# One kernel, three places: order of the prologue's sums, one padded row per channel block in the even convolution, and layer norm and rotation in one stage

## The chip, the core and the metric

The kernel runs on one core of one Trainium2 chip. The metric is the time of one launch in microseconds, as the device counts it. The core has five engines that work side by side and meet at semaphores: TensorE (PE: matmuls), VectorE (DVE), ScalarE (ACT), GpSimd (POOL) and SyncE (SP, which here only issues DMAs).

## What is computed

Two models of two layers each run one after the other on the same latent sequence (512 tokens of width 1024; the first model has 256 context tokens besides). The change touches only what comes ahead of the first layer's attention. In the reference that is:

```python
def layer_norm(x, g, b):
    xf = x.astype(F32)
    mu = jnp.mean(xf, axis=-1, keepdims=True)
    var = jnp.mean(jnp.square(xf - mu), axis=-1, keepdims=True)
    y = (xf - mu) * lax.rsqrt(var + EPS)
...
def conformer_conv(p_glu, conv_w, conv_b, ln_g, ln_b):
    a, gate = jnp.split(p_glu, 2, axis=-1)
    u = depthwise_conv(a * jax.nn.sigmoid(gate), conv_w, conv_b)
    return jax.nn.silu(layer_norm(u, ln_g, ln_b))
...
def even_mixer(h_lat, h_ctx, rope, w_in, ...):
    p_lat = h_lat @ w_in
    conv_lat = conformer_conv(p_lat[..., :EV_Q0], conv_w, conv_b, ln_g, ln_b)
    q_lat = apply_axial_rope(qk_heads(p_lat[..., EV_Q0:EV_K0]), rope)
    k_lat = apply_axial_rope(qk_heads(p_lat[..., EV_K0:EV_V0]), rope)
    v_lat = v_heads(p_lat[..., EV_V0:])
...
    conv_ctx = conformer_conv(p_ctx[..., :EV_Q0], conv_w, conv_b, ln_g, ln_b)
```

The depthwise convolution has 31 taps and 512 channels, and runs over the 512 latent tokens and over the 256 context tokens apart, each padded with zeros. The other part that matters is independent of the tokens: filters of the second layer's long convolution (`hyena_filters`: two small matmuls with sines, a third matmul, a decay and a division by the sum of magnitudes).

## The kernel before

Channels lie on the 128 partitions and tokens along the free dimension, so 512 channels are four blocks `c`. The program is a row of stages. A stage is a block of instruction streams, one for each engine; at its end all engines meet at a barrier, and inside it they meet only at semaphores. Each engine runs its own stream strictly in the order written, so an instruction that waits holds up all behind it on its engine. There is no planner: the order is the order of the code.

**Prologue** (`prologue`, line 1172, until 149.3 us of the trace). TensorE transposes the tokens, and between transposes it makes the filters: `filter(pe, u)`, line 1078, for u = 0 to 15, two matmul instructions into one of two banks. For each u VectorE multiplies by the decay (L1093), ScalarE takes magnitudes (L1106) and VectorE adds them up (L1116); GpSimd adds and subtracts pairs of filters (L1124). Filter u waits until VectorE has taken filter u - 2. Eight squares of the input follow, one for each block of 128 of the 1024 channels: ScalarE squares one into `squares` (L1259, two slots), and TensorE sums it over channels (`sum_blocks`, L518). In the loop over c the order is: square c, then magnitude 6 + c on ScalarE; sum c, then filter 6 + c on TensorE. `first.multiply` (L863) makes the first modulation products from weights in a ring of three tiles.

**Convolution stage** (`products`, called by `even_mixer`, until 368.2 us). TensorE multiplies the normed input by w_in in 20 units of weights, in float32 by three products of rounded halves. For each unit VectorE rounds the weights (`high`, L329), GpSimd makes the rest (`low`, L398), and TensorE waits for `low` (L458); VectorE converts two units ahead. Units 0 to 7 are value and gate of the four channel blocks, 8 to 15 q and k, 16 to 19 v. On odd units from 3 on TensorE also does a piece of modulation (L863, L876). The function `convolve` is called on VectorE once in each unit, and in units 2 to 18 it does 15 of the 248 steps of the convolution: for each block 31 taps, each in two instructions (L788: source times weight plus accumulator; L791 for the first), one for the latent row `pad_lat` (512 wide) and one for the context row `pad_ctx` (256 wide). The two rows take turns, so that a tap waits for the instruction two before it.

**Norm and rotation.** `layer_norm_silu` (L1516 to L1554) is one stage: sums over channels by TensorE, mean and centring by VectorE, squares by ScalarE, their sums, root and reciprocal, scaling and SiLU. Then a stage loads three tables (perm, cos, sin), and `swap_rotate` is another one: for each of eight items (four blocks of q, four of k, 512 wide) TensorE swaps partners with a matmul by `perm` (L1351) and VectorE does x = x cos + swapped sin in three instructions (L1360, L1361, L1362), of which each waits for the one before. The attention stage (L1403 on) follows at 423.8 us.

## Time and profile before

| | us |
|---|---|
| median of three runs | 4256.18 (4255.96 to 4268.26) |
| the profiled execution: time of the run | 4263.13 |
| the profiled execution: span | 4261.3 |
| TensorE busy / VectorE busy / ScalarE busy / GpSimd busy | 3766.9 / 2068.4 / 868.2 / 1400.6 |
| prologue | 0 to 149.3 |
| start of the products to the end of the convolution | 149.3 to 368.2 |
| norm, table loads, rotation | 368.2 to 423.7 |
| all that the change leaves as it is | 423.7 to 4261.3 |

The span begins with the first instruction and ends with the last; the run's own time is 1.8 us more. TensorE is busy for 88% of the span, so over the whole program it is the engine to look at, but the stretches that the change touches are a tenth of the span and have limits of their own. A share of busy time says nothing of them. The trace is read there stage by stage: what the engine that closes the stage waited for last.

### The profile page before, as it was taken

Reading aid. Unit: us, or ns where it says so; the run is one execution under the profiler, and the core shown is the slowest. Engines: PE = TensorE matmul, PEld = TensorE weight load, DVE = VectorE, ACT = ScalarE, POOL = GpSimd, SP = SyncE. Lnnn points to the kernel's source line nnn. Section 1 sums busy time; section 2 is a strip of 40 time slices with the busy share of each in tenths; the row PEclk is TensorE's granted clock in tenths of the full one; section 3 lists DMA queues with packets and bytes.
Section 4 is the critical chain, followed back from the end, with each engine's and each line's share of the span. In section 5 each row is a group of like instructions: output and inputs, shape, how many; then the busy total and the mean of one; then the engine's idle time right before and its main releaser. Section 6 shows DMA issues by size and latency. Waiting matters only on the chain. (4 is left out here: it accounts for less than half of the span.)

```text
span 4261.3 us, 46015 instructions
## 1 busy us (share of the span) xinstructions
PE 3766.9 (88%) x18394; PEld 2961.1 (69%) x18394; DVE 2068.4 (49%) x3150; ACT 868.2 (20%) x1681; POOL 1400.6 (33%) x606
## 2 busy tenths in 40 slices
PE   5896878999989889976999899968999888889998
PEld 2584357888878678845878566757888566667887
DVE  2697644224447456655233467845123377753122
ACT  2211412110011233311100244421000344501001
POOL 1221015225554200004455322225445322245444
PEclk9998969999999979988999899989999899989999
DMA  3440601221213100011333121113332221123332
GB/s 109 150 156 28 235 30 55 63 61 55 69 46 89 47 1 1 1 60 59 99 94 99 54 81 45 45 50 89 95 94 79 65 67 50 30 74 89 99 94 70
DMA packets 400355, 306.83 MB, mean 72 GB/s; under 512 B 11228, under 2 KB 367782, under 8 KB 399559
## 3 DMA queue, kind: packets, MB, share of 16 engines
q1 hardware_dynamic: 397896, 303.11, 23.6%
q8 instruction: 149, 2.44, 0.2%
q10 hardware_dynamic: 2239, 0.71, 0.1%
q14 instruction: 71, 0.58, 0.0%
HBM read 297.48 MB, written 6.29 MB: 71 GB/s over the span
## 5 line engine op out<-in xcount | busy, mean ns | idle before, releaser
L398 POOL TENSOR_TENSOR low<-raw,high 128x1024 fp32r<-128x1024 f32 (+1 forms) x437 | 1058.8, 2424 | 1398.6 <-DVE high L329 1398.6
L458 PE MATMUL scores<-high 128*128 128x512 f32 (+1 forms) x2496 | 962.0, 385 | 123.4 <-POOL low L398 106.8
L458 PE MATMUL scores<-low,high 128*128 128x512 f32 (+1 forms) x2496 | 947.7, 380 | 0.0
L458 PE MATMUL scores<-high,low 128*128 128x512 f32 (+1 forms) x2496 | 945.6, 379 | 0.0
L329 DVE CAST high<-raw 128x1024 fp32r<-128x1024 f32 (+1 forms) x437 | 415.7, 952 | 689.5 <-PE scores L458 374.5
L458 PE MATMUL bank<-high 128*128 128x512 f32 (+1 forms) x1760 | 648.5, 368 | 3.4 <-POOL low L398 3.4
L458 PE MATMUL bank<-low,high 128*128 128x512 f32 (+1 forms) x1760 | 648.1, 368 | 0.0
L458 PE MATMUL bank<-high,low 128*128 128x512 f32 (+1 forms) x1760 | 647.3, 368 | 0.0
L458 PEld LDWEIGHTS scores<-high 128*128 128x128 f32 x2496 | 481.3, 193 | 229.9 <-POOL low L398 116.0
L458 PEld LDWEIGHTS scores<-high,low 128*128 128x128 f32 x2496 | 479.9, 192 | 90.1
L458 PEld LDWEIGHTS scores<-low,high 128*128 128x128 f32 x2496 | 481.9, 193 | 85.5 <-issue 0.5
L458 PEld LDWEIGHTS bank<-high 128*128 128x128 f32 x1760 | 331.8, 189 | 63.3 <-POOL low L398 3.8
L458 PEld LDWEIGHTS bank<-high,low 128*128 128x128 f32 x1760 | 331.6, 188 | 56.1
L458 PEld LDWEIGHTS bank<-low,high 128*128 128x128 f32 x1760 | 332.0, 189 | 55.2
L677 ACT ACTIVATE raw<-x_all 128x512 f32<-128x512 f32 (+1 forms) x64 | 42.1, 681 | 1310.1 <-POOL low L398 1235.3
L351 POOL TENSOR_TENSOR low<-mix,high 128x1536 fp32r<-128x1536 f32 (+1 forms) x6 | 27.0, 4504 | 708.7 <-DVE high L340 708.7
L1592 DVE TENSOR_TENSOR hid<-hid 128x512 f32<-128x512 f32 x96 | 62.3, 649 | 329.9 <-ACT hid L1588 329.9
L351 POOL TENSOR_TENSOR low<-hid,high 128x1024 fp32r<-128x1024 f32 (+2 forms) x36 | 146.6, 4073 | 201.8 <-DVE high L340 201.8
L788 DVE SCALAR_TENSOR_TENSOR conv<-pad_lat,params,conv 128x512 f32<-128x512 f32 x120 | 99.4, 828 | 0.0
L788 DVE SCALAR_TENSOR_TENSOR conv<-pad_ctx,params,conv 128x256 f32<-128x256 f32 x120 | 76.0, 633 | 0.0
L1484 DVE TENSOR_REDUCE mx<-scores 128x1 f32<-128x768 f32 (+1 forms) x48 | 37.2, 775 | 74.6 <-PE scores L1403 74.5
L687 POOL TENSOR_TENSOR raw<-raw 128x512 f32<-128x512 f32 (+1 forms) x40 | 57.1, 1428 | 29.6 <-ACT raw L677 26.6
(575 smaller groups left out, 4350.3 us busy)
## 6 DMA issues: line engine op xcount, KB each, us to landing
raw<-in_mlp_w SPq DMA_DIRECT2D x128, 512.0 KB, 4.0
raw<-in_w_in SPq DMA_DIRECT2D x76, 512.0 KB, 3.9
ring<-in_ada_w SPq DMA_DIRECT2D x32, 1024.0 KB, 7.1
raw<-in_w_gate SPq DMA_DIRECT2D x44, 512.0 KB, 3.9
raw<-in_w_up SPq DMA_DIRECT2D x44, 512.0 KB, 3.9
raw<-in_w_down SPq DMA_DIRECT2D x40, 512.0 KB, 3.5
mix<-in_ada_w SPq DMA_DIRECT2D x16, 1024.0 KB, 7.3
raw<-in_od_w_in SPq DMA_DIRECT2D x29, 512.0 KB, 3.9
```

Source lines behind the costliest of these rows:

```text
L329: dve.tensor_copy(tile(high, u), tile(raw, u)).then_inc(high_ready, 1)
L351: return eng.tensor_tensor(low_, act, high, ALU.subtract)
L398: pool.tensor_tensor(tile(low, u), tile(raw, u), tile(high, u).bitcast(F32), ALU.subtract)\
L458: mm = pe.matmul(out(p), stationary, moving, start=(k0 + k == 0 and i == 0), stop=(k0 + k == job.kc - 1 and i == len(pairs) - 1))
L677: act.activation(self.tile(c), self.x[:, c, 0:self.width], ACT.Square).then_inc(self.squared, 1)
L687: pool.tensor_tensor(self.tile(0), self.tile(0), self.tile(c), ALU.add).then_inc(self.added, 1)
L788: ins = dve.scalar_tensor_tensor(out=out, in0=part, scalar=w[:, j:j + 1], in1=out, op0=ALU.mult, op1=ALU.add)
L1484: step(dve.tensor_reduce(mx[:, u % 2, mp:mp + 1], scores(mp), AX.X, ALU.max))
L1592: return dve.tensor_tensor(hid[:, c, t0:t0 + tn], hid[:, c, t0:t0 + tn], hid[:, c, t0:t0 + tn], ALU.mult)
```

## The change

**Prologue.** `squares` gets six slots where it had two. ScalarE takes magnitude u first and then squares block u - 6; TensorE makes filter u first and sums block u - 8. The first modulation product stands after filter 10 and not after filter 13.

**Convolution.** Latent and context rows of a channel block lie in one padded row, `pad`: 15 zeros, 512 tokens, 30 zeros, 256 tokens, 15 zeros. One instruction does a tap over 798 elements (the 30 between the rows are computed too and used by nobody). Even taps accumulate in `conv`, odd ones in `odd_taps`, and a last addition joins them: 32 steps for each block, 128 in all, 8 for each unit, in units 2 to 17. Odd taps read a copy of the row that ScalarE has shifted by one element (new class `ShiftedRows`: four copies of 826 elements, in units 1, 5, 9 and 13, two slots that lie in the room of v). For that reason the first write of v waits until the convolution has ended.

**Norm and rotation.** `norm_and_rotate` replaces both functions and the stage that loaded tables. SyncE loads the tables while the norm runs. GpSimd does x cos (eight operations), VectorE the other two of each item, and the items are put into gaps of the norm: three swaps ahead of the sums of squares, five behind. The norm works on rows of 798 with zeros in the gap of mean and reciprocal root.

The core of the diff:

```diff
@@ prologue
-        squares = tok[:, 0:2, 0:TA]
+        squares = tok[:, :, 0:TA]
...
-                for c in range(DC):
-                    if c >= 2:
-                        act.wait_ge(x_summed, c - 1)
-                    act.activation(squares[:, c % 2, :], x[:, c, :], ACT.Square).then_inc(x_squared, 1)
-                    hyena_filters.magnitudes(act, NT + c)
-                for u in range(NT + DC, FilterSpectra.N):
+                for u in range(NT, FilterSpectra.N):
                     hyena_filters.magnitudes(act, u)
+                    c = u - NT
+                    if c < DC:
+                        if c >= NT:
+                            act.wait_ge(x_summed, c - NT + 1)
+                        act.activation(squares[:, c % NT, :], x[:, c, :], ACT.Square).then_inc(x_squared, 1)
...
-                for c in range(DC):
-                    pe.wait_ge(x_squared, c + 1)
-                    sum_blocks(pe, m, squares[:, c % 2, :], (LAT, CTX), c == 0, c == DC - 1).then_inc(x_summed, 1)
-                    hyena_filters.filter(pe, NT + c)
-                first.multiply(pe, 0)
-                hyena_filters.filter(pe, NT + DC)
-                hyena_filters.filter(pe, NT + DC + 1)
+                for u in range(NT, FilterSpectra.N):
+                    hyena_filters.filter(pe, u)
+                    if u == NT + 4:
+                        first.multiply(pe, 0)
+                    c = u - NT - 2
+                    if c >= 0:
+                        pe.wait_ge(x_squared, c + 1)
+                        sum_blocks(pe, m, squares[:, c % NT, :], (LAT, CTX), c == 0, c == DC - 1).then_inc(x_summed, 1)
                 first.multiply(pe, 1)
@@ norm_and_rotate
+    segs = ((0, T), (T + GAP, TC))
...
+            issue(sp, [(perm[:, :], A["c_perm_e"]), (cos[:, :], A["c_cos_e"]), (sin[:, :], A["c_sin_e"])], tables_loaded)
...
+            for i, x in enumerate(items):
+                pool.wait_ge(swapped, i + 1)
+                pool.tensor_tensor(x, x, cos[:, :], ALU.mult).then_inc(weighed, 1)
...
+            def swap(i):
+                if i >= 2:
+                    pe.wait_ge(partners_weighed, i - 1)
+                pe.matmul(m.bank[4 + i % 2][:, :], perm[:, :], items[i], start=True, stop=True).then_inc(swapped, 1)
...
+            def weigh_partner(i):
+                dve.wait_ge(swapped, i + 1)
+                if i >= 2:
+                    dve.wait_ge(rotated, i - 1)
+                dve.tensor_tensor(part[:, i % 2, :], m.bank[4 + i % 2][:, :], sin[:, :], ALU.mult)\
+                    .then_inc(partners_weighed, 1)
+
+            def rotate(i):
+                dve.wait_ge(partners_weighed, i + 1)
+                dve.wait_ge(weighed, i + 1)
+                dve.tensor_tensor(items[i], items[i], part[:, i % 2, :], ALU.add).then_inc(rotated, 1)
...
@@ ShiftedRows.scalar
+        c = (u - 1) // 4
+        if u % 4 == 1 and c < 4:
+            if c == 0:
+                act.wait_ge(self.free, 32)
+            elif c >= 2:
+                act.wait_ge(self.convolved, self.steps * (c - 1))
+            self.stored(act, 2 * c + 1, 0, 1)
+            n = self.rows.shape[2]
+            act.activation(self.rows[:, c % 2, :], self.pad[:, c, 1:1 + n], ACT.Copy).then_inc(self.shifted, 1)
@@ even_mixer
+                        def values(act, c, b, y):
+                            if b == 0:
+                                act.wait_ge(copies.convolved, len(steps))
+                            return act.activation(v[:, b, :], y, ACT.Copy)
...
-                        steps = [(c, n) for c in range(4) for n in range(2 * CW)]
+                        steps = [(c, n) for c in range(4) for n in range(CW + 1)]
...
+                                base, acc = (CW + 1) * c, (conv[:, c, :], odd_taps[:, :])
+                                at = min(n, CW - 1)
+                                src = shifted[:, c % 2, at - 1:at - 1 + TG] if at % 2 else pad[:, c, at:at + TG]
...
+                                elif n < CW:
+                                    dve.wait_ge(convolved, base + n - 1)
+                                    ins = dve.scalar_tensor_tensor(out=acc[n % 2], in0=src, scalar=w, in1=acc[n % 2],
+                                                                   op0=ALU.mult, op1=ALU.add)
+                                else:
+                                    dve.wait_ge(convolved, base + n)
+                                    ins = dve.tensor_tensor(acc[0], acc[0], acc[1], ALU.add)
```

What stands in a row on TensorE in the prologue, from the last but one sum on, before (L1078 is a filter, L518 a sum, L863 a modulation product, L1131 the sum of magnitudes):

```order
L518 MATMUL scores<-tok,ones 32x128 x6
L1078 MATMUL scores<-hy_w_102,hy_hid 128x512
L863 MATMUL bank<-ring,cond 32x512 x8
L1078 MATMUL scores<-hy_w_102,hy_hid 128x512 x2
L863 MATMUL bank<-ring,cond 32x512 x8
L1131 MATMUL bank<-hy_total,ones 128x512
```

and after the change, from filters 5 to 8 on (L1080 is a filter, L520 a sum, L865 a modulation product):

```order
L1080 MATMUL scores<-hy_w_102,hy_hid 128x512 x4
L520 MATMUL scores<-tok,ones 32x128 x6
L1080 MATMUL scores<-hy_w_102,hy_hid 128x512
L520 MATMUL scores<-tok,ones 32x128 x6
L1080 MATMUL scores<-hy_w_102,hy_hid 128x512
L865 MATMUL bank<-ring,cond 32x512 x8
```

The sums now stand two filters behind, and the first modulation product has moved up. On VectorE one unit of the convolution stage has, before, a weight conversion (L329) and then pairs of the two rows:

```order
L329 CAST high<-raw 128x1024
L791 TENSOR_SCALAR conv<-pad_lat,params 128x512
L791 TENSOR_SCALAR conv<-pad_ctx,params 128x256
L788 SCALAR_TENSOR_TENSOR conv<-pad_lat,params,conv 128x512
L788 SCALAR_TENSOR_TENSOR conv<-pad_ctx,params,conv 128x256
```

and after it (L331 is the conversion):

```order
L331 CAST high<-raw 128x1024
L1780 TENSOR_SCALAR conv<-pad,params 128x798
L1785 TENSOR_SCALAR odd_taps<-qkv,params 128x798
L1788 SCALAR_TENSOR_TENSOR conv<-pad,params,conv 128x798
L1788 SCALAR_TENSOR_TENSOR odd_taps<-qkv,params,odd_taps 128x798
```

Where a unit had 15 such steps it has 8 wider ones. On VectorE in the norm, before:

```order
L1530 TENSOR_SCALAR mean<-scores 128x512
L1530 TENSOR_SCALAR mean<-scores 128x256
L1534 TENSOR_TENSOR conv<-conv,mean 128x768 x4
L1538 RECIPROCAL rstd<-rstd 128x512
L1538 RECIPROCAL rstd<-rstd 128x256
L1541 TENSOR_TENSOR conv<-conv,rstd 128x768 x4
```

and after it:

```order
L1554 TENSOR_TENSOR conv<-conv,mean 128x798 x4
L1539 TENSOR_TENSOR part<-bank,sin 128x512 x2
L1545 TENSOR_TENSOR qkv<-qkv,part 128x512
L1539 TENSOR_TENSOR part<-bank,sin 128x512
L1545 TENSOR_TENSOR qkv<-qkv,part 128x512
L1561 RECIPROCAL rstd<-rstd 128x512
L1561 RECIPROCAL rstd<-rstd 128x256
L1565 TENSOR_TENSOR conv<-conv,rstd 128x798 x4
L1539 TENSOR_TENSOR part<-bank,sin 128x512
```

Five of VectorE's sixteen rotation steps stand between centring and reciprocal, eleven behind the scaling; none of them is the product with cos, which is GpSimd's now.

## Rows read from the trace of the kernel before

**Rows 1.** Windows: stretch, busy us of each engine (instructions), TensorE clock, DMA share, GB/s

```profile
52.70:102.20 49.50, 31.90 (x133) 10.34 (x132) 14.08 (x23) 12.16 (x18) 11.48 (x8) 1.00 0.08 27
235.00:368.20 133.20, 125.32 (x719) 100.49 (x718) 133.16 (x211) 16.00 (x30) 32.76 (x12) 1.00 0.35 111
368.20:423.70 55.50, 27.36 (x48) 10.93 (x48) 29.95 (x36) 10.88 (x12) 0.00 (x0) 0.73 0.03 11
380.00:385.00 5.00, 3.95 (x5) 1.85 (x6) 0.12 (x1) 2.26 (x3) 0.00 (x0) 0.50 0.00 0
```

**Rows 2.** Timeline of PE, prologue: start us, us, what [idle before <-releaser]

```profile
55.05 1.07 PE L518 MATMUL scores<-tok,ones 128*32 128x128 f32 x12 [2.27 <-ACT tok L1259]
...
60.30 1.07 PE L518 MATMUL scores<-tok,ones 128*32 128x128 f32 x12 [2.18 <-ACT tok L1259]
...
94.78 3.64 PE L863 MATMUL bank<-ring,cond 128*32 128x512 f32 x16
...
98.35 3.78 PE L1078 MATMUL scores<-hy_w,hy_hid 64*128 64x512 f32 x4
```

**Rows 3.** Timeline of ACT, the same stretch

```profile
58.88 0.63 ACT L1106 ACTIVATE qkv<-hy_filt 128x512 f32<-128x512 f32 x1 [3.98 <-DVE hy_filt L1093]
59.42 0.83 ACT L1259 ACTIVATE tok<-x_all 128x768 f32<-128x768 f32 x1
```

**Rows 4.** Tile conv, 180 to 370 us: count, duration ns min/median/max, starts, forms

```profile
L788 DVE SCALAR_TENSOR_TENSOR conv<-pad_lat,params,conv x120: 732/740/2894, 190.5 to 366.9; 128x512 f32<-128x512 f32 x120
L788 DVE SCALAR_TENSOR_TENSOR conv<-pad_ctx,params,conv x120: 468/474/2622, 191.2 to 367.6; 128x256 f32<-128x256 f32 x120
...
L791 DVE TENSOR_SCALAR conv<-pad_lat,params x4: 532/536/543, 187.7 to 327.2; 128x512 f32<-128x512 f32 x4
```

**Rows 5.** Timeline of all engines around one and the last weight conversion

```profile
212.83 0.69 DVE L329 CAST high<-raw 128x1024 fp32r<-128x1024 f32 x1 [1.24 <-DMA raw<-in_ev_w_in]
...
213.61 2.83 POOL L398 TENSOR_TENSOR low<-raw,high 128x1024 fp32r<-128x1024 f32 x1 [12.91 <-DVE high L329]
...
214.10 2.62 DVE L788 SCALAR_TENSOR_TENSOR conv<-pad_ctx,params,conv 128x256 f32<-128x256 f32 x1
...
353.19 0.68 DVE L329 CAST high<-raw 128x1024 fp32r<-128x1024 f32 x1
```

**Rows 6.** Waits of PE, 183 to 368 us: us in total, times, longest

```profile
PE scores L458 <- POOL low L398: 5.5, 4, 1.8
```

**Rows 7.** Timeline of PE and DVE, norm stage

```profile
368.97 7.09 PE L1516 MATMUL scores<-conv,ones 128*128 128x512 f32 x16 [3.18 <-PEq L79]
...
381.05 8.26 PE L1522 MATMUL scores<-sq,ones 128*128 128x512 f32 x16 [4.99 <-ACT sq L1547]
...
376.56 3.56 DVE L1534 TENSOR_TENSOR conv<-conv,mean 128x768 f32<-128x768 f32 x4
...
388.35 5.14 DVE L1538 RECIPROCAL rstd<-rstd 128x512 f32<-128x512 f32 x2 [8.22 <-ACT rstd L1550]
...
393.52 3.57 DVE L1541 TENSOR_TENSOR conv<-conv,rstd 128x768 f32<-128x768 f32 x4
```

**Rows 8.** Timeline of PE and DVE, rotation, and PE's first row of attention

```profile
403.39 3.75 PE L1351 MATMUL scores<-qkv,perm 128*128 128x512 f32 x4 [14.07 <-PEq L79]
...
407.67 1.12 PE L1351 MATMUL scores<-qkv,perm 128*128 128x512 f32 x2 [0.53 <-DVE qkv L1362]
...
406.19 0.69 DVE L1361 TENSOR_TENSOR qkv<-qkv,cos 128x512 f32<-128x512 f32 x1
...
423.77 2.94 PE L1403 MATMUL scores<-qkv 64*128 64x512 f32 x8 [4.08 <-PEq L79]
```

**Rows 9.** Timeline of POOL in the prologue, and of DVE beside a POOL operation

```profile
53.59 2.87 POOL L1124 TENSOR_TENSOR mix<-hy_filt 128x512 f32<-128x512 f32 x2 [4.94 <-DVE hy_filt L1093]
...
163.76 1.39 DVE L605 SCALAR_TENSOR_TENSOR mix<-x_all,gain,bank 128x512 f32<-128x512 f32 x2
...
163.25 1.74 POOL L638 TENSOR_TENSOR low<-mix,high 128x512 fp32r<-128x512 f32 x1
```

More of the change, by code:

```diff
@@ L35 @@
 CW = 31
+GAP = 2 * (CW // 2)
+TG = T + GAP + TC
 HY_FFN = 64
@@ L1339, in _ @@
                                                   in1=small.norm_g[:, 0, :], op0=ALU.add, op1=ALU.mult))
-def swap_rotate(nc, m, items, perm, cos, sin, n_rows):
-    with buffers(nc, part=[P, 2, T]) as part, \
-            stage(nc, "swapped", "chain") as (block, swapped, chain):
-        @block.tensor
-        def _(pe):
-            for i, x in enumerate(items):
-                if i >= 2:
-                    pe.wait_ge(chain, 3 * (i - 1))
-                pe.matmul(m.bank[i % 2][0:n_rows, :], perm[:, :], x, start=True, stop=True)\
-                    .then_inc(swapped, 1)
-        @block.vector
-        def _(dve):
-            step = Chain(dve, chain)
-            for i, x in enumerate(items):
-                y = part[0:n_rows, i % 2, :]
-                dve.wait_ge(swapped, i + 1)
-                step(dve.tensor_tensor(y, m.bank[i % 2][0:n_rows, :], sin[:, :], ALU.mult))
-                step(dve.tensor_tensor(x, x, cos[:, :], ALU.mult))
-                step(dve.tensor_tensor(x, x, y, ALU.add))
 def diff_attention(nc, m, q, k, v, neg_lam, o, queries, keys, side=None):
@@ L1518, in _ @@
                 mm.then_inc(summed, 1)
+            pe.wait_ge(tables_loaded, 48)
+            for i in range(3):
+                swap(i)
             pe.wait_ge(squared, 4)
@@ L1524, in _ @@
                 mm.then_inc(squares_summed, 1)
+            for i in range(3, len(items)):
+                swap(i)
         @block.vector
         def _(dve):
+            def weigh_partner(i):
[8 more added lines that the diff above has]
+                dve.tensor_tensor(items[i], items[i], part[:, i % 2, :], ALU.add).then_inc(rotated, 1)
             for s, (t0, tn) in enumerate(segs):
@@ L1532, in _ @@
             dve.wait_ge(meant, 2)
+            dve.wait_ge(cleared, 2)
             for c in range(4):
                 dve.tensor_tensor(u[:, c, :], u[:, c, :], mean[:, :], ALU.subtract).then_inc(centred, 1)
-            step = Chain(dve, chain)
+            for i in range(3):
+                weigh_partner(i)
+                if i:
+                    rotate(i - 1)
             for s, (t0, tn) in enumerate(segs):
                 dve.wait_ge(rooted, s + 1)
-                step(dve.reciprocal(rstd[:, t0:t0 + tn], rstd[:, t0:t0 + tn]))
+                dve.reciprocal(rstd[:, t0:t0 + tn], rstd[:, t0:t0 + tn]).then_inc(inverted, 1)
+            dve.wait_ge(inverted, 2)
             for c in range(4):
@@ L1541, in _ @@
                 dve.tensor_tensor(u[:, c, :], u[:, c, :], rstd[:, :], ALU.mult).then_inc(scaled, 1)
+            for i in range(3, len(items)):
+                weigh_partner(i)
+                rotate(i - 1)
+            rotate(len(items) - 1)
         @block.scalar
@@ L1553, in _, with __init__, with_signals, scalar @@
                 act.wait_ge(scaled, c + 1)
-                act.activation(dst[:, c, :], u[:, c, :], ACT.Silu, scale=g[:, c:c + 1], bias=b[:, c:c + 1])\
-                    .then_inc(done, 1)
+                for (t0, tn), (d0, _) in zip(segs, (LAT, CTX)):
+                    act.activation(dst[:, c, d0:d0 + tn], u[:, c, t0:t0 + tn], ACT.Silu, scale=g[:, c:c + 1],
+                                   bias=b[:, c:c + 1]).then_inc(done, 1)
+class ShiftedRows(Side):
+    SIGNALS = ("rows_shifted",)
+    def __init__(self, free, pad, rows, steps):
+        self.free, self.pad, self.rows, self.steps = free, pad, rows, steps
+    def with_signals(self, signals):
+        self.shifted, = signals
+    def scalar(self, act, u):
+        c = (u - 1) // 4
[7 more added lines that the diff above has]
+            act.activation(self.rows[:, c % 2, :], self.pad[:, c, 1:1 + n], ACT.Copy).then_inc(self.shifted, 1)
 def residual(x, gate):
@@ L1715, in even_mixer @@
+                                ins.then_inc(convolved, 1)
                         products(nc, m, [
@@ L1720, in even_mixer @@
                             Job(w_in, [(2048, 512)], halves, toks,
-                                lambda act, c, b, y: act.activation(v[:, b, :], y, ACT.Copy), rows=NT)],
-                                 beside=convolve, signals=("convolved",), before=before, ring_tiles=3, banks=6,
-                                 sides=[Modulation(
+                                values, rows=NT)],
+                                 beside=convolve, signals=("convolved",), with_signals=convolution_signals, before=before,
+                                 ring_tiles=3, banks=6, sides=[copies, Modulation(
                                      m, A, [(0, n) for n in range(4, 12)],
```

55 lines of the change are left out of this document (35 added, 20 removed).

## The prediction

> **What bounds the kernel now.** I read the busy shares first: TensorE 88%, but the change lies wholly ahead of 423.7 us, so I took the windows of its three stretches [rows 1]. In the prologue's loop (52.7 to 102.2 us) TensorE is busy 31.9 of 49.5 us and VectorE 14.1: no engine bounds it, a chain does. From 235 us to the end of the convolution VectorE is busy all of 133.2 us and TensorE 125.3. From 368.2 to 423.7 us VectorE is busy 30 and TensorE 27 of 55.5 us at a granted clock of 0.73: again a chain. Then I read the timelines for who releases whom, and the waits for what TensorE lacked in the convolution stage. Everything behind 423.7 us keeps its code and should keep its time.
>
> **Prologue, term A.** One turn of the loop takes 60.30 - 55.05 = 5.25 us [rows 2], of which TensorE works 3.0: a sum takes 1.0 (the filter starts that long after it) and a filter 2.0. The rest is its wait of 2.2 us for ScalarE's square, which stands behind the magnitude (0.63) and before it behind VectorE's decay of the filter just made [rows 3]: filter, decay, magnitude, square, sum, filter is one circle. The new order asks only for squares two filters old, and six slots hold them, so the circle is cut. What is next? A filter waits for VectorE two filters back, and VectorE's two operations of this width (0.69 each by the like one in [rows 8]) and ScalarE's 0.63 + 0.83 fit into 3.0 us. So I take TensorE's own work from 52.7 us: filters 6 to 8 at 1.9 (two back to back took 3.78 [rows 2]) are 5.7, seven more at 2.0 are 14, seven sums at 1.0 are 7, the modulation product 3.6: 30.3 us, and filter 15 ends at 83.0. Before it ended at 98.35 + 3.78 = 102.1. A = 19.1 us. The moved product brings its two DMAs of 1 MB forward by some 30 us, which only frees the ring earlier; the products behind it keep their distances. Bounds: if each of the ten turns held half a GpSimd pair (1.43 of 2.87 [rows 9]), VectorE's two and ScalarE's two operations one after the other, 4.3 us, A would be 49.4 - 43 = 6.4; at most it is 20.
>
> **Convolution, term B.** A tap now costs 0.740 and 0.474 us in two instructions [rows 4]. Per element that is (0.740 - 0.474) / 256 = 1.04 ns, so 798 elements are 0.474 + 542 x 1.04 ns = 1.04 us. Instructions overlap by 0.08 at their ends, so one of them moves the next by 0.955. The trace has no row as wide; the bounds are 0.91 (a smaller fixed part) and 1.06 (the two old ones). The first two taps of a block are of the kind that took 0.54 for 512 elements, some 0.65 here, and the join takes 1.0. A block of 32 steps is 2 x 0.65 + 29 x 0.955 + 1.0 = 30.0 us, so a unit's 8 steps take 7.5. Now a unit: from one conversion to the thirteenth after it there are 353.19 - 212.83 = 140.4 us, 10.80 each [rows 5]. Of these 0.6 is the conversion, 2.15 a stop (the context tap took 2.62 instead of 0.47 while GpSimd made its `low` [rows 5]), 0.1 the bias, and 7.95 fifteen steps. So each unit gets 0.45 shorter, 10.35. TensorE needs only 9.81 a unit, but it ran ahead of VectorE until 292 us and lacked `low` for 5.5 us in all after that [rows 6]. Thirteen units times 0.45 is 5.9, so nearly all of the 5.5 comes back, and no more: TensorE ends at 365.8 - 5.4 = 360.4. Before, the stage ended with VectorE at 368.2, since its steps ran on into unit 18; now they end at 347.4 + 0.6 + 7.5 + 2.15 = 357.6. The added wait, v's copies until then, holds six ScalarE operations of 0.6 that end by about 361.1, with nothing queued behind them. The four shifted copies (826 elements, under 0.9 us each) lie in ScalarE's idle time (16 of 133 us busy [rows 1]); the first ends just as VectorE's first tap does and may cost 0.2. B = 368.2 - 361.1 = 7.0 us, with bounds 3 (taps of 1.0) and 8.
>
> **Norm and rotation, term C.** Before: from 368.97 to 423.77 is 54.8 us [rows 7, 8], with 28.1 to the end of scaling (393.52 + 3.57), 6.3 from there to the first swap (SiLU's end, tables, barriers), and eight items of three VectorE operations of 0.7, each waiting for the one before. I count the new stage from TensorE's start. Sums until 7.1; the tables, loaded from 0 on, have landed by then, since all of those 6.3 us held them. Centring starts at 7.6. Four wide subtractions of 0.92 would end at 11.3. But GpSimd now has two items to weigh (1.43 each, half of 2.87 [rows 9]), and here the lock matters: VectorE operations with both inputs in SBUF stood still for a GpSimd operation [rows 5], while two with one input in PSUM ran on beside one (1.39 us for two [rows 9]). Centring reads SBUF twice, so 2.9 us are added: 14.1. Then weigh_partner(0) to 14.8, and TensorE's third swap, after idling, at the lower clock (0.50, which is 1.2 of 2.4 GHz, in the same place before [rows 1]): 3.75 / 2 = 1.87 us, to 16.7 [rows 8]. The sums of squares start there; before, the root of the first was done 7.3 us after their start [rows 7]; part of the slow spell is now spent on the swap, so 6 us, 22.7. Reciprocals 5.14, to 27.8. Scaling 3.65, to 31.5 (items 3 and 4 are weighed during the reciprocals). Then eleven VectorE operations and three GpSimd ones that lock out the five additions among them: 11 x 0.7 = 7.7, three stops of 0.7 to 0.8, so 10.0: 41.5, and 0.9 to attention's first matmul: 42.3. C = 54.8 - 42.3 = 12.5 us. SiLU in eight pieces ends long before. Bounds: 9.5 (both slow spells in full, the tail's swaps at 1.87) and 16.5 (no lock).
>
> The Trainium skill, SBUF — State Buffer, section "Who interferes with whom", says that VectorE and GpSimd share one pair of ports under an exclusive lock, held for a whole instruction. That speaks against giving cos to GpSimd: it takes 1.43 us for what VectorE does in 0.69. By the lock C is 12.5, without it 16.5, and the trace agrees with the lock.
>
> **Sum.** 19.1 + 7.0 + 12.5 = 38.6 us. Against the profiled run of 4263.1 us that is 4224.5; the run lies 7 us above the median of 4256.2, one of the three runs at 4268.3 even 12, and the median gives **4217.6 us, say 4218**.
>
> **Rivals.** (1) *No lock in the rotation*: 4214; against it stands the tap of 2.62 us. (2) *The prologue's loop stays bound, by VectorE and GpSimd*: A is 6.4, the time 4230; for it speaks that GpSimd's pairs now come every 6 us and can lock out additions, against it that VectorE has only 1.4 us of work in 3.0. (3) *The clock gives it back*: TensorE enters attention at the lower clock (the first eight score matmuls took 2.94 us [rows 8], about half of it the clock's); if idling in the rotation's tail keeps it there 10 us longer, or the run is one of the long ones, 8 to 12 us are lost: 4228. (4) *Slower: the wide tap*. A unit is 2.85 + 8p with p the pace of a tap. At 0.994 it equals today's 10.80, and each further 0.1 costs 13 x 0.8 = 10.4 us. Against A + C = 31.6 the change breaks even at p = 1.30 and is over 0.3% slower from 1.42. It would give 4270. It needs a cost that grows faster than the width, for reading three streams (row, shifted copy, accumulator) or for the slots in v's room; the two widths in rows 4 grow by 1.04 ns an element with hardly any spread between minimum and median, for even and odd taps alike, which speaks against it, and also says that the shifted copies buy no speed of their own. (5) *The change doesn't do what it says*: the copies on ScalarE wait for a signal that comes late (the spectra's store) and VectorE stops: the old code asked for that store only in unit 8, the new one in unit 1, 50 us earlier by the pace of the units; a late landing would cost under 10 us, 4226.
>
> **How the numbers follow.** Forecast 0.66; (1) 0.08; (2) 0.07; (3) 0.12; (4) 0.04, half of it in between (a tap near 1.2, 4245); (5) 0.03. Within 0.3% (12.8 us, about what a measurement of this kernel can tell from no change) lie half of (4) and the far end of (3) with (2): same 0.04, slower 0.02, faster 0.94. The bounds of the terms sum to gains of 19 to 44, but they will not all fall on one side; with (1) below and (2) and (3) above, the range is 4206 to 4236.
>
> **What would show it.** Right: turns of 3.0 us in the prologue and filter 15 at 83; wide taps 0.95 us apart; TensorE without a wait for `low` of over 0.5 us; attention at 423.8 - 38.6 = 385. For the lock: centring over 6 us in place of 3.6, with GpSimd's products inside it, and additions of 1.4 us in the tail. Wrong: taps over 1.06, a prologue loop whose idle time has VectorE as releaser, or a difference behind attention's start of more than 5 us.

## The result and the profile after

The changed kernel takes 4210.6 us (median of 4 runs, 4207.2 to 4211.3), the kernel before 4257.2 in the same comparison. The ratio is 0.9881, with a 95% interval of 0.9867 to 0.9896: 1.2% faster, 46.6 us between the medians. The forecast was 4218 with a range of 4206 to 4236: faster, as forecast, but by 8 us more than its sum of 38.6. The profiled execution took 4211.3 us.

Between the two traces three instructions mark the stretches: the last small turn of the prologue on TensorE, the norm's first matmul, and attention's first matmul.

| | before | after | gained | forecast |
|---|---|---|---|---|
| last turn of the prologue | 145.86 | 118.67 | A 27.2 | 19.1 |
| from there to the norm | 223.1 | 214.5 | B 8.6 | 7.0 |
| from the norm to attention | 54.8 | 37.2 | C 17.6 | 12.5 |
| from attention to the end | 3837.5 | 3839.2 | -1.7 | 0 |

That is 51.8 us between the traces. The profiled execution of before lay 5.9 us above its median here and that of after 0.6, which leaves 46.5. In which of the four stretches those 5.3 us lie, the traces don't show.

The prologue's loop on TensorE, after (start us, duration, what), to be held against [rows 2]:

```profile
61.31 1.07 PE L520 MATMUL scores<-tok,ones 128*32 128x128 f32 x12
62.31 2.07 PE L1080 MATMUL scores<-hy_w,hy_hid 64*128 64x512 f32 x2
64.31 3.64 PE L865 MATMUL bank<-ring,cond 128*32 128x512 f32 x16
67.73 1.05 PE L520 MATMUL scores<-tok,ones 128*32 128x128 f32 x12
68.71 1.12 PE L1080 MATMUL scores<-hy_w,hy_hid 64*128 64x512 f32 x2
69.76 0.63 PE L520 MATMUL scores<-tok,ones 128*32 128x128 f32 x12
70.32 1.12 PE L1080 MATMUL scores<-hy_w,hy_hid 64*128 64x512 f32 x2
```

No line names idle time: the circle is cut, and a turn takes 3.0 us, as forecast. But from the one at 68.71 us on the same filter takes 1.12 us where it took 2.07, and a turn 1.61. The windows (stretch, busy us of each engine, then TensorE's clock) say why:

```profile
58.00:64.00 6.00, 6.00 (x29) 2.14 (x28) 3.74 (x7) 3.53 (x6) 2.84 (x2) 0.50 0.01 4
64.00:68.00 4.00, 4.00 (x25) 1.05 (x26) 1.29 (x2) 1.36 (x2) 0.00 (x0) 0.50 0.19 19
68.00:76.00 8.00, 8.00 (x70) 3.23 (x62) 5.38 (x8) 4.65 (x7) 5.36 (x4) 0.96 0.68 252
```

The granted clock stands at 0.50 (1.2 GHz) until 68 us and at 0.96 on the mean of the next 8 us, so it rises to 1.00 (2.4 GHz) early in them. The same column stood at 1.00 in the first line of [rows 1], where every filter took 2.07 us as well: in that trace the column did not tell the clock of this stretch, and the duration of a known instruction did.

The convolution, by tile (duration in ns: minimum, median, maximum), against [rows 4]; then what TensorE waited for from 150 to 331 us, against [rows 6]:

```profile
L1788 DVE SCALAR_TENSOR_TENSOR conv<-pad,params,conv x60: 1034/1037/3182, 162.3 to 327.1; 128x798 f32<-128x798 f32 x60
L1788 DVE SCALAR_TENSOR_TENSOR odd_taps<-qkv,params,odd_taps x56: 1033/1039/3191, 163.2 to 326.2; 128x798 f32<-128x798 f32 x56
```

```profile
PE scores L460 <- POOL low L400: 1.1, 1, 1.1
```

A wide tap takes 1.04 us, as worked out, for either parity. Thirteen conversions lie 135.7 us apart, from 182.93 to 318.66, 10.44 a unit (forecast 10.35, before 10.80). TensorE waits for `low` once, 1.1 us, and not five times. The stage ends with v's copies, as forecast.

The norm and the rotation, after (timeline; in brackets idle time ahead and its releaser), against [rows 7, 8]:

```profile
333.15 5.40 PE L1518 MATMUL scores<-conv,ones 128*128 128x512 f32 x16 [1.33 <-PEq L81]
...
339.05 5.83 DVE L1554 TENSOR_TENSOR conv<-conv,mean 128x798 f32<-128x798 f32 x4
...
339.56 3.57 POOL L1507 TENSOR_TENSOR qkv<-qkv,cos 128x512 f32<-128x512 f32 x2 [6.27 <-PE bank L1514]
...
345.53 2.08 PE L1514 MATMUL bank<-qkv,perm 128*128 128x512 f32 x2 [5.27 <-DVE part L1539]
...
347.40 5.89 PE L1527 MATMUL scores<-sq,ones 128*128 128x512 f32 x16
...
364.39 1.25 DVE L1545 TENSOR_TENSOR qkv<-qkv,part 128x512 f32<-128x512 f32 x1
...
370.33 2.94 PE L1383 MATMUL scores<-qkv 64*128 64x512 f32 x8 [3.88 <-PEq L81]
```

GpSimd's two products lie inside the centring, which takes 5.83 us instead of about 3.7: the lock, as forecast. The same shows in an addition of 1.25 us (0.68 for the same addition at 346.00, beside which GpSimd is idle).

### The profile page after: what moved, and what is told of

It is laid out like the page before. It is cut to its first block and busy times, and to the rows that moved or that the text cites. A ratio compares the mean times of both kernels' runs of the same rounds, so it can differ in the third digit from the quotient of the medians.

```text
span 4209.5 us, 45870 instructions
## 1 busy us (share of the span) xinstructions
PE 3750.4 (89%) x18394; PEld 2959.2 (70%) x18394; DVE 2054.6 (49%) x3022; ACT 872.7 (21%) x1689; POOL 1418.6 (34%) x615
## 5 line engine op out<-in xcount | busy, mean ns | idle before, releaser
L331 DVE CAST high<-raw 128x1024 fp32r<-128x1024 f32 (+1 forms) x437 | 417.3, 956 | 689.2 <-PE scores L460 376.4
L1788 DVE SCALAR_TENSOR_TENSOR odd_taps<-qkv,params,odd_taps 128x798 f32<-128x798 f32 x56 | 77.4, 1382 | 0.0
L1464 DVE TENSOR_REDUCE mx<-scores 128x1 f32<-128x768 f32 (+1 forms) x48 | 37.2, 776 | 72.6 <-PE scores L1383 72.5
L1788 DVE SCALAR_TENSOR_TENSOR conv<-pad,params,conv 128x798 f32<-128x798 f32 x60 | 66.6, 1110 | 0.0
```

The lines of the kernel that those rows point to most:

```text
L331: dve.tensor_copy(tile(high, u), tile(raw, u)).then_inc(high_ready, 1)
L1464: step(dve.tensor_reduce(mx[:, u % 2, mp:mp + 1], scores(mp), AX.X, ALU.max))
L1788: ins = dve.scalar_tensor_tensor(out=acc[n % 2], in0=src, scalar=w, in1=acc[n % 2], op0=ALU.mult, op1=ALU.add)
```

## The experiments

**after_again**: the changed kernel once more, as a base for the later comparisons.

> The changed kernel as it is, beside the kernel before on this chip, so that the runs of this call have a common base. Ratio to before 0.988 to 0.990, as in the first comparison (0.9881).

Measured: 0.9880 (0.9864 to 0.9897). The same three marks in its trace give A 27.0, B 7.4 and C 15.4 us, and the rest of the program 5.6 us longer than before. So A comes out as in the first trace, and C, for the same code, 2.2 us smaller. From attention to the end, where no version changes the code, the fourteen traces lie between 3829.5 and 3846.7 us; the 1.7 us in the table are no measurement of an effect there.

All ratios are to the kernel before, run on the same chip in the same comparison, with 95% intervals; 0.001 is 4.3 us. The next seven ask where the 8 us of term A come from.

**order_only**: the kernel before with the prologue's part of the diff and nothing else.

> The kernel before with the prologue's part of the change alone (six squares, sums two filters behind, first modulation product after filter 10). Theory CLOCK: the new order leaves TensorE without a pause, and the granted clock rises from 1.2 to 2.4 GHz inside the loop, as the trace of the changed kernel shows at 67.7 us (a filter takes 1.12 us there and 2.07 before). Then the prologue gives about 27 us, the median is about 4230, and the last eight filters take 1.1 us each. Rival ORDER: the cut circle is worth what it is at the old pace, 19 us, and the other 8 us of the trace belong to something else in the changed kernel: 4238, filters at 2.07 throughout.

Measured: 0.9931 (0.9915 to 0.9948), 29 us faster, with 22 to 36 in the interval. The last turn comes at 120.22 (before 145.86), so 25.6 by the traces. The clock rose inside the loop here too:

```profile
65.14 2.86 PE L863 MATMUL bank<-ring,cond 128*32 128x512 f32 x16
67.83 0.60 PE L518 MATMUL scores<-tok,ones 128*32 128x128 f32 x12
68.36 1.12 PE L1078 MATMUL scores<-hy_w,hy_hid 64*128 64x512 f32 x2
```

So A belongs to the prologue's part, and by the durations of the filters and sums some 8 us of it to the clock. What lifted the clock was still only argued.

**busy_gaps**: does a pause keep it down? The order of before, and its pauses filled.

```diff
                     hyena_filters.filter(pe, NT + c)
+                    if c < DC - 1:
+                        pe.matmul(m.bank[6][:, :], hyena_filters.hid[:, 1, 0:P], hyena_filters.w3[:, 0:512],
+                                  start=True, stop=True)
```

> The kernel before, order unchanged, with one useless matmul (64x128 by 64x512, 2.07 us at the lower clock) on TensorE behind each of the filters 6 to 12, in the 2.2 us in which it waits for the next square. It reads the filter's own operands and writes a bank that nobody reads. Theory CLOCK: the pauses alone kept TensorE at 1.2 GHz; with them filled the clock rises after about as long a busy stretch as in the changed kernel (16 us), a turn of the loop falls from 5.25 to about 3.85 us (filter and sum shorter by 0.95 and 0.45), and the kernel with more work is 4 to 10 us faster: 4246 to 4252. Rival ORDER: the clock has nothing to do with the pauses; turns stay at 5.25 us or a little over, 4256 to 4258.

Measured: 0.9996 (0.9983 to 1.0009). Turns stay at 5.25 us, all at the lower clock, though TensorE is idle for only 0.47 us in each. A miss for CLOCK as put there; but 0.47 us were left. Behind the loop, though, the modulation product at 95.93 us is shortened (3.43 us), and the two filters behind it take 1.98 us, where the kernel before has 3.78 [rows 2].

**no_pauses**: the same with two such matmuls ahead of each wait for a square (`pe.wait_ge(x_squared, c + 1)`).

> The kernel before, order unchanged, with two useless matmuls (64x128 by 64x512 each, 3.8 us together at the lower clock) ahead of TensorE's wait for each of the eight squares, so that no pause is left from 33 us on, not even the 0.5 us a turn that the run with one of them kept. Theory CONTINUITY: the clock rises once TensorE has worked without any pause for about as long as in the changed kernel (from 33.7 to 67.7 us there). Turns are 6.8 us until then (2 or 3 of them, +1.5 each) and 3.85 to 4.0 after it (5 or 6, -1.3 each), and the 7 us of work behind the loop that ran at the lower clock take half: 6 to 9 us faster than before. Theory PRODUCT: it is the modulation product (128 rows, 512 wide) that lifts the clock; then all eight turns are 6.8 us and the kernel is 12 us slower than before.

Measured: 1.0016 (1.0005 to 1.0027), 7 us slower (PRODUCT had said 12, with turns of 6.8 us; they took 6.41). TensorE has no pause from 34 to 110 us, and in the whole loop nothing rises. The rise comes with the product behind it: two filters in a row take 1.98 us after it. The last of the eight turns, the product and those two filters:

```profile
98.41 3.62 PE L1293 MATMUL bank<-hy_w,hy_hid 64*128 64x512 f32 x4
101.96 1.07 PE L518 MATMUL scores<-tok,ones 128*32 128x128 f32 x12
102.96 2.07 PE L1078 MATMUL scores<-hy_w,hy_hid 64*128 64x512 f32 x2
104.96 3.55 PE L863 MATMUL bank<-ring,cond 128*32 128x512 f32 x16
108.44 1.98 PE L1078 MATMUL scores<-hy_w,hy_hid 64*128 64x512 f32 x4
```

That work without a pause is enough to lift the clock, my first reading of the trace, is refuted. The Trainium skill, TensorE: Matmul & The Clock Gate, section "Part 1: The HAM clock gate (the "warmup" mystery)", has the low clock as the resting state and activity of TensorE as what releases it. Here the two agree only in part: over 70 us of filters, sums and transposes without a pause did not release it, and the measurement decides.

**product_late**: the changed kernel with `if u == NT + 7:` for `if u == NT + 4:`, which puts the first modulation product behind filter 13.

> The changed kernel with the first modulation product back behind filter 13 (it stands behind filter 10 in the changed kernel). Theory CONTINUITY: the clock rises at 67 to 68 us all the same, in the middle of filters and sums, and the time is that of the changed kernel within 1 us. Theory PRODUCT: the clock rises only with the product, which now starts at about 73 us at the lower clock; three more turns cost 3.0 instead of 1.6 us, and the time is 4 to 5 us longer.

Measured: 0.9892 (0.9873 to 0.9912). The total can't be told from 0.988, the trace can: the filter at 70.79 still takes 2.07 us, the product is shortened on its way, and all behind it is fast. The last turn of the prologue comes at 121.36 us, 2.7 us later than in the changed kernel, where PRODUCT had said 4 to 5.

```profile
70.79 2.07 PE L1080 MATMUL scores<-hy_w,hy_hid 64*128 64x512 f32 x2
72.79 2.94 PE L865 MATMUL bank<-ring,cond 128*32 128x512 f32 x16
75.56 0.60 PE L520 MATMUL scores<-tok,ones 128*32 128x128 f32 x12
```

The rise moved with the product. In ten of the eleven traces with the new order (this one and those told below included) it comes 2 to 5 us after the product's start, worked out from how far the product or the instructions behind it are shortened; the exception follows.

A product is not the only work behind which the clock rises. In the changed kernel TensorE begins at 23.20 us, after a wait of 13.71 us, with a small matmul and transposes, and then:

```profile
25.97 1.88 PE L1277 MATMUL scores<-ident,tok 128*128 128x128 f32 x8
29.48 1.12 PE L1080 MATMUL scores<-hy_w,hy_hid 64*128 64x512 f32 x2 [1.64 <-ACT hy_hid L1070]
33.72 1.94 PE L1277 MATMUL scores<-ident,tok 128*128 128x128 f32 x8 [3.12 <-ACT x_all L1237]
```

The filter at 29.48 us runs at the higher clock right behind transposes, and in the pause behind it the granted clock falls back to 0.50. Eight traces have this early rise; in five, that of the kernel before among them, this filter takes 2.07 us. So PRODUCT holds inside the loop, as an observation; why the rise follows the product there, and not the filters, sums and transposes, no run shows.

**product_first** and **product_first_2**, the same code run twice:

```diff
+                first.multiply(pe, 0)
                 for u in range(NT, FilterSpectra.N):
                     hyena_filters.filter(pe, u)
-                    if u == NT + 4:
-                        first.multiply(pe, 0)
```

> The changed kernel with the first modulation product ahead of filter 6 instead of behind filter 10; nothing else. Its weights have landed by 37 us in the trace of the changed kernel. Theory PRODUCT (the 128-row matmuls of the modulation product, and not the lack of pauses, lift the clock, as the run with a late product showed, where it rose at 75.5 and not at 68 us): the clock rises within 5 us of the product's start at about 52, so at 57 instead of 68 to 69; the 11 us of TensorE's work between are done in 6, and filter 15 ends at about 71 instead of 76.3 to 77: 5 us faster than the changed kernel, 0.9865 to 0.987 of the kernel before. Rival: the clock rises only at about 68 whatever work comes first; then nothing changes (0.988). One row speaks against PRODUCT alone: in the kernel before, the product at 94.78 was followed by 3.8 us of filters at the lower clock.

> The same kernel as product_first once more. Its profiled execution took 4225.2 us and shows the whole loop at the lower clock (filter 15 ends at 85.0), while its other runs took 4202 to 4216. Theory BY EXECUTION: whether and when the clock rises in the loop differs between executions of the same code, and the time of the run tells it: an execution of about 4202 to 4208 has the clock up before 68 us and ends filter 15 at 71 to 77 us, one of 4215 to 4225 has it late or not at all in the loop. Rival PLACE: a product this early never lifts the clock; every profile of this kernel shows the loop at the lower clock and filter 15 at 85, and the spread of the times has another cause.

Measured: 0.9871 (0.9854 to 0.9887; single runs from 4202 to 4225 us) and 0.9880 (0.9862 to 0.9898; 4207 to 4214). The two profiled executions, of 4225.2 and 4211.7 us, part at the product. The first:

```profile
53.42 3.64 PE L865 MATMUL bank<-ring,cond 128*32 128x512 f32 x16
56.99 5.49 PE L1080 MATMUL scores<-hy_w,hy_hid 64*128 64x512 f32 x6
...
81.40 2.07 PE L1080 MATMUL scores<-hy_w,hy_hid 64*128 64x512 f32 x2
```

and the second:

```profile
53.14 3.01 PE L865 MATMUL bank<-ring,cond 128*32 128x512 f32 x16
56.08 3.03 PE L1080 MATMUL scores<-hy_w,hy_hid 64*128 64x512 f32 x6
...
69.94 1.12 PE L1080 MATMUL scores<-hy_w,hy_hid 64*128 64x512 f32 x2
```

BY EXECUTION holds in its first half: one product, one place, and in one execution the clock rises within it, at 55 us, in the other not before 89 us. Whether the time of a run tells it, as the expectation said, is open: 4211.7 us lies between its two bands. The product makes a rise likely and does not assure it; the product at 94.78 in [rows 2], followed by 3.8 us of filters at the lower clock, is the same case. In both the next product brings the rise: in product_first that at 85.41, 4 us after its start, and in the kernel before that at 104.06, after 3 us, by these lines (the sum of magnitudes, L1131, takes 2.07 us at the lower clock):

```profile
104.06 3.31 PE L863 MATMUL bank<-ring,cond 128*32 128x512 f32 x16 [1.93 <-ACT flat L884]
107.29 1.12 PE L1131 MATMUL bank<-hy_total,ones 128*128 128x512 f32 x2
...
122.08 1.92 PE L863 MATMUL bank<-ring,cond 128*32 128x512 f32 x16
```

So in all fourteen traces the first rise that comes after 50 us comes 2 to 5 us after the start of a modulation product, in twelve of them the first one. What tips it stays open. The first trace is also the measurement of A without the clock: filter 15 ends at 83.5 (from a start 0.7 us later than before), and the last turn comes at 129.2, which makes A 16.7. As a version product_first gains nothing that can be measured: even with its filters done at 71 (second trace), a load (2.97 us of waiting at 96.94) and a slow spell behind it leave the last turn at 117.5, 1.2 us ahead of the changed kernel's, and attention starts no earlier (370.7).

**warm_start**: 21 useless matmuls (`spin`: 128x128 by 128x512, constants, into a bank that nobody reads) while TensorE waits in the first 23 us.

```diff
+                spin(6)
                 hyena_filters.argument(pe, 0)
+                spin(15)
                 hyena_filters.argument(pe, 1)
```

> The changed kernel with 21 useless matmuls (128x128 by 128x512) in the first 23 us of TensorE, where it waits for loads (6 of them) and for the sines (15); they read constants and write a bank that nobody reads. Theory WIDE WORK (128-row, 512-wide matmuls lift the clock and narrower work then keeps it): from about 10 us on one takes 0.54 us instead of 0.94, and filters and transposes behind them run at 2.4 GHz (1.1 and 1.0 us instead of 2.07 and 1.97), so that the clock costs nothing before 68 us: 5 to 9 us faster than the changed kernel. Rival FALLS BACK: the clock rises during them and falls again in the pauses at 28 and 31 us, where transposes wait for ScalarE: no change, 0.988.

Measured: 0.9889 (0.9873 to 0.9906). FALLS BACK. Transposes at 25.65 us take 1.04 instead of about 1.9; after pauses of 2.17 and 2.62 us it is over, and the last turn of the prologue comes at 119.10 us (118.67 in the changed kernel):

```profile
25.65 1.04 PE L1277 MATMUL scores<-ident,tok 128*128 128x128 f32 x8
28.86 1.63 PE L1080 MATMUL scores<-hy_w,hy_hid 64*128 64x512 f32 x2 [2.17 <-ACT hy_hid L1070]
33.10 1.94 PE L1277 MATMUL scores<-ident,tok 128*128 128x128 f32 x8 [2.62 <-ACT x_all L1237]
```

The other four ask for terms B and C. **no_copies**: odd taps read `pad` itself, and `ShiftedRows` and v's wait are gone.

```diff
-                                src = shifted[:, c % 2, at - 1:at - 1 + TG] if at % 2 else pad[:, c, at:at + TG]
+                                src = pad[:, c, at:at + TG]
```

> The changed kernel without the four shifted copies: odd taps read the padded row itself, one element further on, and v is written without waiting for the convolution. Theory WIDTH: what was gained came from one wide instruction in place of two, and the address of a tap is free: odd taps stay at 1.04 us, 0.96 apart, and the time is 4209 to 4212 (v's copies no longer held back may give 1 or 2). Rival ALIGNMENT: an odd start costs something on float32 rows; each 0.1 us on the 60 odd taps is 6 us, so a tap of 1.2 would give 4220 and more.

Measured: 0.9895 (0.9877 to 0.9914), level with the changed kernel. Odd taps, now from `pad`:

```profile
L1782 DVE SCALAR_TENSOR_TENSOR odd_taps<-pad,params,odd_taps x56: 1033/1040/3190, 168.0 to 332.1; 128x798 f32<-128x798 f32 x56
```

1040 ns against 1039: WIDTH. The median of 4219 us stands beside 4264 us for the kernel before in this comparison; on the 4257 us of the first one the ratio gives 4212.5, where WIDTH said 4209 to 4212. Of the 6.3 us that its trace is longer than the changed kernel's, 4.7 arise by the last turn of the prologue, whose code the two share; from there to the norm it takes 215.4 us against 214.5, and the norm and rotation 37.5 against 37.2. The four copies, their slots and the wait buy no speed.

**norm_apart**: the changed kernel with norm, table loads and rotation as three stages again.

> The changed kernel with norm, table loads and rotation apart as before (same code as before, but on rows of 798). It prices the merged stage. By the trace of the changed kernel the merge gave 17.6 us, so the time is 4211 + 17.6 = 4228. By the term of the prediction (12.5 us) it is 4223. The difference between this kernel and order_only is the convolution's term: 7 to 8.6 us by the trace, 7.0 by the prediction.

Measured: 0.9916 (0.9899 to 0.9932), between order_only and the changed kernel. The norm starts at 335.38 and attention at 389.72, 54.3 us, where the merged stage takes 37.2: C is 17.2 by these two traces, and 15.0 against the 39.4 us of after_again. By the ratios it is 0.9916 - 0.9880, 15 us give or take 10. B is the rest: from the last turn to the norm 221.8 us in order_only (120.22 to 342.02) and 215.4 here (119.95 to 335.38), 6.4.

**cos_on_vector**: x cos on VectorE, next to `weigh_partner`, and no GpSimd in the rotation.

```diff
+                dve.tensor_tensor(items[i], items[i], cos[:, :], ALU.mult).then_inc(weighed, 1)
```

> The changed kernel with x cos on VectorE in the merged stage (eight more operations of 0.61 us there, none on GpSimd). By the trace of the changed kernel GpSimd's products stop VectorE for 2.1 us in the centring (5.83 instead of 3.69), about 0.6 in the addition at 348.25 and 2.5 in the tail (additions of 1.25, 1.0 and 1.56 for two), 5.2 us in all. Theory LOCK: VectorE gains these and pays 8 x 0.61 = 4.9, of which the three in the middle (1.8 us) fall beside the sums of squares, where it waits anyway: 2 us faster to 0.5 slower than the changed kernel. Rival NO LOCK (the long operations have another cause): they stay long and the products come on top, 3 to 5 us slower.

Measured: 0.9877 (0.9860 to 0.9894), level. The long operations are gone, centring first:

```profile
343.14 3.69 DVE L1551 TENSOR_TENSOR conv<-conv,mean 128x798 f32<-128x798 f32 x4
...
371.49 0.69 DVE L1542 TENSOR_TENSOR qkv<-qkv,part 128x512 f32<-128x512 f32 x1
```

LOCK holds, and so does its price: in the tail each item takes 2.0 us here and 1.4 to 2.0 in the changed kernel. The whole stage took 39.9 us here, against 37.2 in the changed kernel's trace and 39.4 in that of after_again. The last is the fair comparison: in both the first sums took 7.10 us, at a granted clock of 0.64 to 0.72 in their first 5 us, where the changed kernel's trace has 5.40 us at 1.00. The expectation counted 2.5 us of stops in the tail; held against 0.69 for an addition they are 1.2, so GpSimd stops VectorE for 3.9 us in all, and VectorE's own eight products take 4.9, of which three stand where it would wait anyway. GpSimd's products give back in stops about what they take off VectorE.

**warm_norm**: 15 useless wide matmuls in TensorE's pauses of the merged stage (five ahead of the third swap, seven ahead of the sixth, three at the end).

> The changed kernel with 15 useless matmuls (128x128 by 128x512) in the pauses of TensorE in the merged stage: five ahead of the third swap, seven ahead of the sixth, three behind the last. Theory WARM: the clock stays at 2.4 GHz through the stage and into attention: third swap 1.1 us instead of 2.08, sums of squares 5.4 instead of 5.9, the first eight score matmuls 1.5 instead of 2.94, and the low clock until about 381 us in attention is gone: 3 to 5 us faster than the changed kernel, 0.987. Rival: those stretches wait for VectorE and ScalarE, or the low clock returns in attention's own pauses: within 1 us of the changed kernel, 0.988. If the clock is low already when they start, the five cost up to 1 us.

Measured: 0.9888 (0.9872 to 0.9905), no change, though every step of WARM's mechanism came: third swap 1.12 us, sums of squares 5.32, first score matmuls 1.57.

```profile
348.19 1.12 PE L1514 MATMUL bank<-qkv,perm 128*128 128x512 f32 x2 [0.99 <-DVE part L1548]
349.16 5.32 PE L1533 MATMUL scores<-sq,ones 128*128 128x512 f32 x16
...
372.46 1.57 PE L1383 MATMUL scores<-qkv 64*128 64x512 f32 x8 [2.03 <-PEq L81]
```

The stage takes 36.7 us instead of 37.2, since VectorE and GpSimd set its end. What attention gains at its start is gone later: from its first matmul to the end of the span there are 3839.4 us in this trace and 3839.2 in the changed kernel's. Where it goes is not shown. TensorE's waits for modulation weights from attention's start to 405 us (in all, times, longest) are longer here than in the changed kernel:

```profile
PE bank L865 <- DMA ring<-in_ada_w: 6.8, 5, 1.7
```

```profile
PE bank L865 <- DMA ring<-in_ada_w: 3.2, 4, 1.5
```

But three traces without the useless matmuls there wait 5.8 to 5.9 us in the like stretch (product_first_2, warm_start, cos_on_vector), and from 390 to 400 us the DMA share is 1.04 with them and 1.03 without.

No version tried beats the changed kernel by more than the measurement can tell.

## Why the prediction came out as it did

**What bounds the kernel now**: right. Prologue and norm were chains, the convolution was VectorE's, and what lies behind attention's start moved by 1.7 us in the two traces. That it was so little is luck in part, since that stretch differs by up to 17 us between traces of the same code.

**Term A**: the mechanism was right, and its size at the old clock nearly so. The forecast had filter 15 end at 83.0; product_first's first execution, at the lower clock throughout, has it at 83.5. By the last turn 16.7 of the forecast's 19.1 us are left: besides these 0.5 us, the slower next product and sum of magnitudes cost 0.5 and a slow spell behind a load at 110 us 1.5. The step that failed is "seven more at 2.0 are 14, seven sums at 1.0 are 7": it took durations of the old trace as fixed, where they were those of the lower clock, and the trace of before held the hint (the product of [rows 2] took 3.64 us, the same kind at 122.08 us 1.92). At the higher clock five filters (0.95 each) and five sums (0.44 each) are 7.0 us shorter, and the next product 1.4: with the forecast's 19.1 that makes 27.5, and the trace has 27.2. The bound "at most it is 20" was wrong for the same reason.

**Term B**: 8.6 by the first pair of traces and 6.4 by the second, 7.4 with after_again, forecast 7.0 (its own figures, 368.2 - 361.1, give 7.1). Tap, pace, unit and the end by v's copies were right to 0.1 us each. TensorE kept one wait for `low` of 1.1 us, over the 0.5 said to be the limit.

**Term C**: 17.6 (17.2 by norm_apart, 15.4 with after_again), forecast 12.5. The lock was right, and nearly its size: 2.1 us in the centring for 2.9 forecast. Three more sizes were off. The first sums were taken at 7.1 us and took 5.4; the sums of squares to the root took 4.9 for 6; and the tail 8.6 for 10.0, because GpSimd stopped the additions in it for 1.2 us in all and not 2.2. The first two are the clock again (in the first sums 1.00 in this trace, and 0.62 to 0.71 in the first 5 us before), and they are a chance as well. TensorE idled only 1.3 us ahead of the first sums, where it had idled 3.2 before, and of ten traces with such a short pause (1.0 to 1.3 us) eight have them at 5.40 us; but after_again and cos_on_vector have 7.10, as forecast. The four with a pause of 3.2 us have 7.0 to 7.9. That cos on GpSimd is no better than on VectorE was only half said: the forecast had the lock cost 4 us, and cos_on_vector shows that VectorE's own eight products cost about as much.

**Rivals.** No lock: refuted. A bound loop (A of 6.4): refuted, VectorE was busy 5.4 of 8 us at the fast pace. The clock gives it back: refuted in sign; attention did start at the lower clock, in before as well (2.94 us in both). The wide tap: refuted. Late copies: none; VectorE did not wait for them. (Unit 1 lies further ahead of unit 8 than the 50 us of the forecast: ScalarE's copies in units 1 and 9 start at 158.56 and 232.54 us, which makes some 65 us for seven units.) What was missing was a rival on the clock's other side, a denser stretch in which it rises, with 8 us to give. With it the sum would have been 4210; that this is the measured median is luck in part, since B and C came out 1.6 and 5.1 us larger in the same trace, 5.3 us of the difference between the traces are the draw of the two executions, and after_again has another C.

**Range and spread.** 4210.6 lay within 4206 to 4236, near its low end. The spread among runs of one kernel, up to 23 us in product_first, is in part this same clock: its run of 4225 us lost 11.7 us by the last turn against its run of 4212. Another part arises behind attention's start (3829.5 to 3846.7 us in the fourteen traces); its cause was not looked for.

## What to carry to other kernels

Before a duration goes into a sum, ask at which clock it was taken; compare one known instruction in two places of the trace, and give the other clock a term of its own. When pauses go from a stretch of TensorE, price the shorter chain and the possible rise apart, and treat the second as a chance. A faster stage buys only up to the next resource: useless matmuls made TensorE fast where VectorE and GpSimd set the end of the stage, and bought nothing that could be measured. And take more than one trace of the same code before you explain 2 us: the merged stage took 37.2 us in one and 39.4 in another.

## What the runs showed of the hardware that I had not expected

- TensorE worked from 34 to 105 us without a pause, on filters of 64 rows, sums and transposes, and stayed at the lower clock; it left it within the modulation product that came then (no_pauses). In all fourteen traces the first rise after 50 us came 2 to 5 us after the start of a modulation product, in twelve of them the first such product, and it moved with that product by some 6 us (product_late).
- A short rise can come without a product: in eight traces a filter behind transposes at 29 to 30 us took 1.12 us, in five 2.07.
- The same code had the clock up at 55 us in one execution and at 89 us in another (product_first).
- The clock column of a trace can read 1.00 where instructions run at half pace ([rows 1] and the filters of [rows 2]); in other traces it reads 0.50 for the same stretch.
- An odd start of a float32 row costs VectorE nothing in a tap with two SBUF inputs (1040 against 1039 ns).
- GpSimd's product of 128x512 takes 1.24 to 1.8 us. Eight of them stopped VectorE's two-input operations for 3.9 us in all, where VectorE's own eight products take 4.9. GpSimd's `low` also stops an operation with one SBUF input: the first odd tap at 159.58 us took 2.77 us beside it, the first even tap just ahead 0.69 (forecast 0.65 each).
